# One group of DMA loads moved from GpSimd's queue to ScalarE's

## The reference

```python
def reference(x, ...):
    for l in range(DEPTH):                       # DEPTH = 1
        h = rms_norm(x, ln1_g[l])
        p = h @ w_in[l]
        p_rwkv = token_shift(p[..., :SHIFT_DIM], shift_mu_prev[l], shift_mu_next[l])
        ...
        o_rwkv = rwkv7_bidirectional(...)        # group A
        o_att = windowed_gqa_alibi(...)          # group B, |t-s| <= 128
        x = x + jnp.concatenate([o_rwkv, o_att], axis=-1) @ w_out[l]
        h = rms_norm(x, ln2_g[l])
        gate = depthwise_conv_centred(h @ ffn_w_gate[l], ffn_conv_w[l], ffn_conv_b[l])
        x = x + (jax.nn.gelu(gate, approximate=False) * (h @ ffn_w_up[l])) @ ffn_w_down[l]
    return rms_norm(x, lnf_g)

# inside rwkv7_bidirectional, for both directions z, one token after the other:
    def step(S, inp):
        rt, wt, kt, vt, at, bt = inp             # at = -kk, bt = kk * a
        Sa = jnp.einsum('zbhij,zbhj->zbhi', S, at)
        S = S * wt[..., None, :] + Sa[..., :, None] * bt[..., None, :] + vt[..., :, None] * kt[..., None, :]
        return S, jnp.einsum('zbhij,zbhj->zbhi', S, rt)
```

## Time and profile before

| | |
|---|---|
| median of 3 runs | 1375.43 us (1374.97 to 1379.25) |
| profiled execution | 1381.39 us, its span 1379.4 us |
| PE busy | 1281.8 us, 93% of the span |
| DVE busy | 857.1 us, 62% |
| ACT busy | 521.9 us, 38% |
| POOL busy | 231.2 us, 17% |
| chain that ended last | PE 75%, DVE 11%, DMA 5%, issue 3%, SPq 3%, ACT 2%, POOL 2% |
| mean DMA rate | 130 GB/s over the span |

### The profile page before, as it was taken

One profiled execution on the slowest core, in us unless ns is written; L12 is line 12 of the kernel. 1 busy time (PEld: TensorE's weight loads), 2 busy tenths in 40 slices (PEclk: granted clock), 3 DMA queues, 4 the chain that ended last, 5 costly groups with the idle time before them and its releaser, 6 DMA issues.

```text
span 1379.4 us, 28338 instructions
## 1 busy us (share of the span) xinstructions
PE 1281.8 (93%) x11280; PEld 1001.4 (73%) x11280; DVE 857.1 (62%) x1094; ACT 521.9 (38%) x729; POOL 231.2 (17%) x242
## 2 busy tenths in 40 slices
PE   6999999897589988889999999999999999999997
PEld 2476776775356655567778888888888888888886
DVE  4986687799557777783398555565555573333345
ACT  3735345221246656742144333333333342111221
POOL 1001001021312233400005222222222110000000
PEclk9999999999669989999989999999999999999998
DMA  5038758697666776502313222333222455322103
GB/s 212 20 92 188 173 149 200 182 257 181 162 203 214 237 219 208 173 31 98 131 46 92 76 68 85 91 91 87 66 76 91 137 176 208 114 97 72 49 31 123
DMA packets 145830, 179.53 MB, mean 130 GB/s; under 512 B 52432, under 2 KB 107792, under 8 KB 145776
## 3 DMA queue, kind: packets, MB, share of 16 engines
q1 hardware_dynamic: 136384, 152.16, 36.9%
q0 software_dynamic: 4288, 12.98, 3.4%
q10 hardware_dynamic: 5104, 13.67, 3.1%
HBM read 121.16 MB, written 57.54 MB: 130 GB/s over the span
## 4 chain that ended last, share of the span: by engine, by line
PE 75%; DVE 11%; DMA 5%; issue 3%; SPq 3%; ACT 2%; POOL 2%; DVEq 0%; ACTq 0%; POOLq 0%
PE banks L1107 28%; PE banks L695 18%; PE banks L677 6%; PE banks L1144 5%; PE banks L683 3%; DVE work L1969 2%; DVE work L1973 2%; PE banks L1081 2%; PE banks L659 2%; PE banks L885 2%; PE banks L901 1%; DMA work<-y_d 1%; DMA work<-in_w_in 1%; PE banks L1089 1%; PE banks L975 1%
## 5 line engine op out<-in xcount | busy, mean ns | idle before, releaser
L1107 PE MATMUL banks<-op,sw_hi 128*128 128x512 f32 x1120 | 344.8, 389 | 0.0
L1107 PEld LDWEIGHTS banks<-op,sw_hi 128*128 128x128 f32 x1120 | 210.3, 188 | 43.7
L1107 PE MATMUL banks<-op,sw_lo 128*128 128x512 f32 x560 | 217.8, 389 | 0.0
L2162 DVE TENSOR_TENSOR xT<-xT,banks 128x1024 f32<-128x1024 f32 x23 | 28.1, 1221 | 150.4 <-PE banks L695 150.4
L1107 PEld LDWEIGHTS banks<-op,sw_lo 128*128 128x128 f32 x560 | 105.1, 188 | 21.7
L1477 ACT ACTIVATE sw_hi<-work 128x1024 fp32r<-128x1024 f32 (+1 forms) x60 | 72.1, 1203 | 112.2 <-PE banks L1107 110.1
L1765 DVE TENSOR_TENSOR sw_lo<-work,sw_hi 128x1024 fp32r<-128x1024 f32 (+1 forms) x60 | 84.9, 1416 | 37.5 <-ACT sw_hi L1477 37.5
L677 PE MATMUL banks<-ph_hi,pw_hi 128*128 128x512 f32 x272 | 87.7, 404 | 6.4 <-DVE work L1887 3.1
L1739 POOL TENSOR_TENSOR work<-work 128x512 f32<-128x512 f32 x20 | 28.4, 1418 | 387.0 <-DMA work<-in_w_gu 245.9
L677 PE MATMUL banks<-ph_hi,pw_lo 128*128 128x512 f32 x272 | 86.2, 399 | 0.0
L695 PE MATMUL banks<-g_hi,down_hi 128*128 128x512 f32 x256 | 79.0, 390 | 0.0
(11 more groups left out here) (277 smaller groups left out, 2492.4 us busy)
## 6 DMA issues: line engine op xcount, KB each, us to landing
work<-scan_d SPq DMA_DIRECT2D x32, 768.0 KB, 4.8
work<-in_w_gu SPq DMA_DIRECT2D x88, 256.0 KB, 4.6
scan_d<-work SPq DMA_DIRECT2D x16, 1024.0 KB, 5.3
g_d<-hT SPq DMA_DIRECT2D x22, 512.0 KB, 2.9
scan_d<-work SPq DMA_DIRECT2D x32, 256.0 KB, 6.6
work<-in_w_down SPq DMA_DIRECT2D x16, 512.0 KB, 3.6
work<-in_w_in ACTq DMA_DIRECT2D x15, 512.0 KB, 3.7
work<-g_d SPq DMA_DIRECT2D x15, 512.0 KB, 4.4
```

The costliest lines, as they stand in the source:

```text
L1107: mm = pe.matmul(banks[:, 3 * slot + bank, :], w[:, n, k * P:(k + 1) * P], x[n][:, k, :], start=(opens and k == 0 and p_ == 0), stop=(k == ...
L2162: tt(x, x, product, ALU.add).then_inc(added[slot], 1)
```

## The change

The four DMAs that load the last pair's forward rows (j = 3, z = 0) into `M[0]` are issued by ACT, between `split_hi(1, j + 2)` and the wait for `ab_ready`, with the wait for `G_stored` in front of them. POOL skips this group and issues the other 28. The four raise a semaphore of their own: the parameter load's, renamed from `par_loaded` to `par_then_M`, so that DVE waits for 16 of it at the start and for 16 * 5 before the solve, and for 16 * 12 in place of 16 * 16 of `M_loaded[0]`. Sources, destinations and sizes are the same, and so are all other instructions.

```diff
@@ -1270,6 +1270,13 @@
                 for half, slot in enumerate((0, 3)):
                     keys_out(j, 0, half, slot)
                 split_hi(1, j + 2)
+                if last:
+                    act.wait_ge(s["G_stored"], 32 * j + 16 + FREE)
+                    for e in range(2):
+                        for q in range(2):
+                            act.dma_start(M[0][C * j + q:C * (j + 1):2, e, :, :],
+                                          scan_d[0, :, half_rows(e, q, 0, C), 1, j, 2 * C * q:2 * C * q + C])\
+                                .then_inc(s["par_then_M"], 16)
                 act.wait_ge(s["ab_ready"], 2 * j + 2)
                 if last:
                     act.wait_ge(s["AR_stored"], 16 * (2 * NPAIR - 1) + FREE)
@@ -1637,7 +1644,7 @@
             for j in range(NPAIR):
-                for z in range(2):
+                for z in range(j == NPAIR - 1, 2):
                     pool.wait_ge(s["G_stored"], 32 * j + 16 * (z + 1) + FREE)
@@ -1948,7 +1955,9 @@
             for z in range(2):
                 dve.wait_ge(s["TI_init"], 2 * z + 2)
-                dve.wait_ge(M_loaded[z], 16 * 4 * NPAIR)
+                dve.wait_ge(M_loaded[z], 16 * 4 * (NPAIR - (z == 0)))
+                if z == 0:
+                    dve.wait_ge(s["par_then_M"], 16 * 5)
                 for n in range(1, C):
```

More of the change, by code:

```diff
@@ L301, in hymba_block @@
         assert w.at <= XG_AT + 3 * T
-        names = """consts_loaded par_loaded consts_made xg_ready p_rms
+        names = """consts_loaded par_then_M consts_made xg_ready p_rms
             p_mm p_scaled p_shift1 p_shifted lora_tanh lw_full
@@ L404, in _ @@
                 sp.sem_inc(x, FREE)
-            sp.dma_start(par[:, :], a["par"]).then_inc(s["par_loaded"], 16)
+            sp.dma_start(par[:, :], a["par"]).then_inc(s["par_then_M"], 16)
             sp.dma_start(xT[:, 0, :], a["xT"][:, 0, :]).then_inc(x_loaded[0], 16)
@@ L1791, in _ @@
             dve.memset(eps[:, 1:2], LNX_EPS).then_inc(s["consts_made"], 1)
-            dve.wait_ge(s["par_loaded"], 16)
+            dve.wait_ge(s["par_then_M"], 16)
             mp, mn = par[:, COLS["mu_prev"]:COLS["mu_prev"] + 14], par[:, COLS["mu_next"]:COLS["mu_next"] + 14]
```

## The result

The changed kernel is slower: 1383.28 us median against 1378.32 of the kernel before, both over 14 runs taken side by side, ratio of the timed runs 1.0048, with a 95% interval of [1.0032, 1.0063] (the two medians alone give 1.0036, the two means 1.0046; all three lie in the interval). By that ratio the loss is 6.6 us (0.0048 x 1378), within an interval of 4.4 to 8.7. The profiled execution of the changed kernel took 1387.19 us (span 1385.4), 3.9 above its median; that of before 1381.39.

What follows compares the result with a forecast made beforehand. The prediction took the G rows' relay through DRAM into M, before the last pair's solve, as the bound. DVE reaching `split_lo` 0.4 us sooner, all other terms 0, gave 1375.43 - 0.4 = 1375.0 us, range 1371.8 to 1379.5.

Steps and rivals of the forecast that it cites:

- What bounds the kernel, and the stake: Before the last pair's solve: G rows stored to DRAM and reloaded into M; DVE's 4.65 us wait is the most gainable.
- POOL's four issues are worth 0: POOL's queue: dropping 2.50 us of issues from 262.47 gains nothing, since nobody waits for them.
- ScalarE's issues at 0.5 us each, cost 0: ScalarE before `qkv_out(0)`: four issues end near 264.3, before ScalarE is needed at 267.01, so nothing moves.
- The cover: ScalarE's free time until 267.01, hiding the issues; if it went, `qkv_out(0)`, weight load and `pw_hi` 2.6 us late at most.
- M lands at 269.1, from 2048 rows x (1.8 + 0.9) ns: M loads alternating row for row with SP's stores: 262.3 + 5.5 + 1.3 = 269.1, 0.65 us sooner than 269.75.
- The tail: M's landing behind ScalarE's last issue: 1.3 us, taken from ScalarE's small moves.
- The turns by whole packets: DMA engines alternate between queues by packet, so POOL's bundles get more a turn than 128-byte packets; no size in the forecast.
- The packet counts: Queue totals after the change: ScalarE's q10 at 7216 packets, POOL's q0 at 4160.
- What is late next: DVE after five solve rows: `gram_rows`, then `split_lo` waiting for `pw_hi` until 275.4, leaving 0.4 us of gain.
- Rival 2: ScalarE's M loads stand behind SP's stores: M at 276.3, solve 6.5 us later, 1381.9 us; chance 0.09.
- Rival 1: M's 128-byte packets cost as much as SP's rows: M at 271.0, 1.25 later, +1.2 us, 1376.6; chance 0.19.

Runs made afterwards that it cites:

- late-M run: Kernel before, with POOL made to wait for PE's first late product in front of the last pair's four forward M loads; ratio 1.0065 [1.0040, 1.0091].
- the second profile: The changed kernel run once more with nothing altered (7 runs), against the kernel before; ratio 1.0054 [1.0031, 1.0076].
- spare-load run: Kernel before, M loads still on POOL, plus four ScalarE loads of the same shape into memory nobody reads; ratio 1.0013 [0.9996, 1.0030].

## Why the prediction was wrong

It forecast 1375.0 us, between 1371.8 and 1379.5 on the scale of a 1375.43 us kernel, with 0.85 for no difference and 0.10 for slower. The measured ratio puts it at 1.0048 x 1375.43 = 1382.0, outside that range. Step by step:

- *What bounds the kernel, and the stake.* Right. The relay through DRAM sets the solve's start; start and end move about one for one (late-M run, 0.6 to 1.4 by its interval). The stake was named as 4.65 us of gain at most; on the side of loss it had no such lid, and that is where it went.
- *POOL's four issues are worth 0.* Nothing speaks against it; nothing tested it by itself. One reading in the sum is off: 264.3 is when POOL's last issue starts; its issues end at 262.47 + 2.50 = 264.97.
- *ScalarE's issues at 0.5 us each, cost 0.* Wrong by a factor of three: 6.00 / 4 = 1.50 us, and 1.35 in the second profile. The bounds (0.38 to 1.84) held it. I took the lower end because of the earlier trace rows, a ScalarE issue of 0.34 us in the middle of a long one of SP. That row is of another shape, and the measured first issues are short too (0.74 us): one row couldn't speak for the fourth. With SP's stores held the same four took 0.69 us each. Half of M's delay, 2.0 of 4.0 us, comes in here. The cover was gone by 1.3 us (`qkv_out(0)` at +11.42 instead of +10.08; +10.85 in the second profile, where PE and not the issues ended the wait), and `pw_hi` came at +19.29 instead of +17.36. By the spare-load run this costs at most 0.30%, and 0.13% as measured, which includes M's own delay of some 1.3 us there.
- *M lands at 269.1, from 2048 rows x (1.8 + 0.9) ns.* **This is the step that failed.** The sum allowed 5.5 + 1.3 = 6.8 us from ScalarE's first issue to the landing. Measured are 275.76 - 264.23 = 11.5 us, and 12.0 in the second profile: 4.7 us too little, and M lands at +16.8 where +12.2 was forecast. The assumption was that the M rows take turns with SP's one for one and that the issues don't hold them up. The DMA view shows 3.7 of SP's packets for one of M's, and SP's row at its old 1.6 to 1.8 ns, so that it gave up nothing. The tail behind the end of the last issue was put at 1.3 us, from small moves that didn't run beside SP's stores; it was 275.76 - 270.23 = 5.5. With SP's stores held the whole way is 4.9 us, less than the sum allowed (the tail 2.2), so the term was mis-sized for the company that the rows keep and not for the rows. The turns by whole packets, which the Trainium skill states ("DMA: Bandwidth & Descriptors", section on queues, rings and completion order), have the direction right in the stretch compared: POOL's 2 KB packets moved all of M in 7.4 us, ScalarE's single rows half of it in 6.0. No run changed M's packet size alone, so that this is the reason is argued and not shown. Equal turns, which the sum assumed, aren't what the packet counts show here.
- *The packet counts.* Right to the packet: 7216 and 4160.
- *What is late next.* The order was right (`gram_rows`, then `split_lo` behind `pw_hi`), but for a solve that starts sooner. Nothing was worked out for one that starts later, past saying that every step moves with it. There TensorE's wait for `gram_rows` grows from 3.12 to 4.79 us, its product ends 5.0 us later, and a weight load is late 28 us into the solve. In the profile that is 3.6 of the 7.6 us by which the solve ends later; the forecast had no term for it.
- *Rival 2, with a chance of 0.09, is what happened*, in place and sign, and in size by luck, by two errors that met. It had M at 276.3 and +6.5 us; measured are M at 273.7 (+16.8 us, on the time axis of before's profile) and +6.6 us. M landed 2.6 us sooner than it said, and the wait at step 19, which it didn't have, adds an amount that the runs don't settle. Rival 1 (packets lose, M 1.25 us later) had the right sign and a third of the delay.

Open is why ScalarE's second to fourth issues take 1.3 to 1.9 us. It isn't the number of packets (5.23 us with a quarter of them) and isn't the queue alone (2.76 us with SP silent). Nor is it that SP is issuing: in the changed kernel SP's last issue ends at 266.81 + 1.52 = 268.33, and the fourth load's issue, the longest with 1.86 us, starts behind it; the weight load's at 270.44 takes 1.19 us where it took 0.33, with the engines as full in both. What these cases share is that ScalarE's own earlier rows had not yet been moved. That fits, and no run tests it by itself. And of the 0.48%, 0.34 is M's delay by the late-M run's rate; the other 0.14 is within the interval.

## What to carry to other kernels

When a load on the critical path moves to another queue, count its packets on the new queue and ask who else has rows in flight in that stretch: a load that is short in a quiet stretch (2.7 us) took 6.5 beside another queue's small rows, and an issue went from 0.69 to 1.5 us. What helps is that the competing rows come later. Here it was done in two ways with the same start of the solve: the loads in the competing engine's own queue, ahead of its stores (+11.1 to +11.4), or the stores held while POOL loads (+11.0). Neither is shown to make the kernel faster than before, so look first at what the held rows hold up themselves. And price a later landing as carefully as an earlier one: here the gain had a lid of 4.65 us and the loss had none.

## What the runs showed of the hardware that was not expected

- Beside SP's stores of 256-byte rows, ScalarE's 128-byte rows got one packet for 3.7 of SP's (1006 to 3749 in 6.0 us; one for 3.1 in the second profile). Alone, with the same loads and SP's stores held, 2112 packets passed in 5.0 us at a DMA share of 0.34:

```profile
q10 hardware_dynamic: 2112, 0.26, 33.6%
```

- A ScalarE issue of 512 rows takes 0.64 to 0.73 us in a quiet stretch. With SP's stores on the engines the first takes 0.74 and those behind it up to 1.86 us (2.12 among the spare loads), also after SP's last issue has ended. POOL's issues of the same loads took 0.63 us in both cases; their landings went from 2.4 to 4.7 us with the stores, and to 7.5 when issued 5.0 us later.
- A later start of the solve reaches TensorE's product behind `gram_rows`. After waits of 1.41, 3.12, 4.79 and 11.10 us (second and first profile of before, changed, late-M) the lowest granted clock of the six-microsecond stretches in which the product runs was 1.00, 0.75, 0.62 and 0.50 (0.50 is the 1.2 GHz level throughout), and the product took 11.2, 12.9, 13.9 and 13.1 us. The wait alone doesn't order them all: in the spare-load kernel the last wait was 0.20 us and the clock of that stretch 0.86 (276 to 282 us).
